# Later join and cache loads on GpSimd's queue in the attention stage of a decoder step

## The reference

```
for g in range(3):                       # (window, dilation) = (128, 1), (512, 4), (2048, 16)
    s = q_g . k_g * scale - slope * distance        # 129 keys per query, strided by the dilation
    m = max(s);  p = exp(s - m);  l = sum(p)
    o_g = p . v_g / l;  lse_g = m + log(l)
alpha = softmax over g of lse_g
o_a = sum over g of alpha_g * o_g                   # this is "the join"
```

## Time and profile before

| | us |
|---|---|
| median of 3 runs (3123.8 to 3127.46) | 3126.55 |
| the profiled execution | 3124.32 |
| span of its instructions | 3122.5 |
| TensorE busy in the span | 2919.9 (94%) |
| VectorE, ScalarE, GpSimd busy | 1361.6, 1085.1, 836.7 |

### The profile page before, as it was taken

One profiled execution on the slowest core, in us unless ns is written; L12 is line 12 of the kernel. 1 busy time (PEld: TensorE's weight loads), 2 busy tenths in 40 slices (PEclk: granted clock), 3 DMA queues, 4 the chain that ended last, 5 costly groups with the idle time before them and its releaser, 6 DMA issues. The chain is left out here.

```text
span 3122.5 us, 47274 instructions
## 1 busy us (share of the span) xinstructions
PE 2919.9 (94%) x18020; PEld 2609.9 (84%) x18020; DVE 1361.6 (44%) x3061; ACT 1085.1 (35%) x2165; POOL 836.7 (27%) x704
## 2 busy tenths in 40 slices
PE   7889999999999899999999999995979889589999
PEld 7778998888888799999999999993656656389999
DVE  2584334566544233343565645422434334433333
ACT  1343213444444333212444444442534434221110
POOL 0242333555422222232555533210011112040000
PEclk9999999999999999999999999997989797799999
DMA  6364432332322432322333232227676776353432
GB/s 195 95 178 137 125 95 77 105 98 92 104 99 88 166 113 94 111 84 88 95 100 102 90 100 94 98 71 263 240 262 224 254 246 212 123 194 109 126 119 86
DMA packets 385264, 417.90 MB, mean 134 GB/s; under 512 B 115600, under 2 KB 296080, under 8 KB 378384
## 3 DMA queue, kind: packets, MB, share of 16 engines
q1 hardware_dynamic: 378128, 406.24, 41.0%
q10 hardware_dynamic: 6912, 8.65, 0.8%
HBM read 284.11 MB, written 130.70 MB: 133 GB/s over the span
## 5 line engine op out<-in xcount | busy, mean ns | idle before, releaser
L667 PE MATMUL weave_bank<-h_high,w_high 128*128 128x352 f32 (+2 forms) x2240 | 819.8, 366 | 15.2 <-issue 11.4
L669 PE MATMUL weave_bank<-h_high,w_low 128*128 128x352 f32 (+2 forms) x2240 | 801.4, 358 | 0.0
L668 PE MATMUL weave_bank<-h_low,w_high 128*128 128x352 f32 (+2 forms) x2240 | 799.1, 357 | 0.0
L944 POOL TENSOR_TENSOR w_low<-weave_w_raw,w_high 128x512 fp32r<-128x512 f32 x284 | 379.9, 1349 | 771.1 <-ACT w_high L815 769.2
L667 PEld LDWEIGHTS weave_bank<-h_high,w_high 128*128 128x128 f32 x2240 | 427.0, 191 | 57.5 <-issue 14.7
L669 PEld LDWEIGHTS weave_bank<-h_high,w_low 128*128 128x128 f32 x2240 | 426.0, 190 | 40.4
L668 PEld LDWEIGHTS weave_bank<-h_low,w_high 128*128 128x128 f32 x2240 | 426.0, 190 | 39.7 <-issue 2.9
L679 PE MATMUL weave_bank<-w_high,h_high 128*128 128x256 f32 x1088 | 310.0, 285 | 0.0
L681 PE MATMUL weave_bank<-w_high,h_low 128*128 128x256 f32 x1088 | 306.7, 282 | 0.0
L680 PE MATMUL weave_bank<-w_low,h_high 128*128 128x256 f32 x1088 | 305.6, 281 | 0.0
L1671 ACT ACTIVATE mix_probs<-mix_scores,mix_o_out 128x256 f32<-128x256 f32 (+1 forms) x384 | 157.0, 454 | 319.2 <-DVE mix_o_out L1754 307.1
(11 more groups left out here) (229 smaller groups left out, 4860.6 us busy)
## 6 DMA issues: line engine op xcount, KB each, us to landing
weave_w_raw<-in_w_qkv SPq DMA_DIRECT2D x144, 256.0 KB, 2.9
mix_kv<-in_kT_c SPq DMA_DIRECT2D x24, 1024.0 KB, 7.6
mix_kv<-in_v_c SPq DMA_DIRECT2D x24, 1024.0 KB, 7.1
tail_gates<-scratch_gates SPq DMA_DIRECT2D x48, 352.0 KB, 3.2
weave_w_raw<-in_w_g SPq DMA_DIRECT2D x64, 256.0 KB, 3.0
weave_w_raw<-in_w_b SPq DMA_DIRECT2D x60, 256.0 KB, 2.8
scratch_sums<-mix_o_out SPq DMA_DIRECT2D x48, 264.0 KB, 6.0
mix_rows<-scratch_sums SPq DMA_DIRECT2D x24, 528.0 KB, 6.8
```

Source lines behind the costliest of these rows:

```text
L667: pe.matmul(dst, w_high[:, i, k, :], h_high[:, k, tok], start=(k == 0), stop=False)
L668: pe.matmul(dst, w_high[:, i, k, :], h_low[:, k, tok], start=False, stop=False)
L669: mm = pe.matmul(dst, w_low[:, i, k, :], h_high[:, k, tok], start=False, stop=(k == KD - 1))
L944: pool.tensor_tensor(w_part(w_low, p), w_raw[p % RAW][:, :, :], w_part(w_high, p), ALU.subtract).then_inc(w_low_done, 1)
```

## The change

Three things change in `phase_mix`. The parts of the samples all stand four blocks later (`at` begins at 8 in place of 4). For half 0 of the first three head pairs everything behind `load_rows` stands five blocks later (`later`), the load itself where it was. And `load_stage` moves from SP's list, unchanged, to GpSimd's: stages 0 and 1 at the top of the stage, right behind the clearing of the semaphores, the others in a loop over the blocks in which the weighted sums stand at their blocks.

```
-    at = lambda i, k: 4 + SPAN * i + k * SPAN // PARTS
+    at = lambda i, k: 8 + SPAN * i + k * SPAN // PARTS
...
-    turn_at = lambda jp, half: start(jp, half) + (12 if jp < PAIRS - 1 else 6 + 2 * half)
+    later = lambda jp, half: 5 if jp < PAIRS - 1 and half == 0 else 0
+    turn_at = lambda jp, half: start(jp, half) + later(jp, half) + (12 if jp < PAIRS - 1 else 6 + 2 * half)
     J_LOAD = {start(*x): x for x in J_HALVES}
-    J_LEAST = {start(*x) + 2: x for x in J_HALVES}
-    J_EXP = {start(*x) + 3: x for x in J_HALVES}
-    J_WEIGHT = {start(*x) + 4: x for x in J_HALVES}
-    J_SUM = {start(*x) + (7 if x == (PAIRS - 1, 1) else 5): x for x in J_HALVES}
+    J_LEAST = {start(*x) + later(*x) + 2: x for x in J_HALVES}
+    J_EXP = {start(*x) + later(*x) + 3: x for x in J_HALVES}
+    J_WEIGHT = {start(*x) + later(*x) + 4: x for x in J_HALVES}
+    J_SUM = {start(*x) + later(*x) + (7 if x == (PAIRS - 1, 1) else 5): x for x in J_HALVES}
...
             def _(sp):
-                def load_stage(s): ...
...
-                load_stage(0)
-                load_stage(1)
                 for n in range(END):
...
-                    if n in S_LOAD:
-                        load_stage(S_LOAD[n])
...
             def _(pool):
+                def load_stage(s): ...          # as before, with pool.wait_ge and pool.dma_start
...
                 nc.clear_and_free_semaphores(t["used"])
-                for jp in range(PAIRS - 1):
-                    for half in range(2):
-                        weighted_sums(pool, jp, half)
+                load_stage(0)
+                load_stage(1)
+                for n in range(END):
+                    if n in S_LOAD:
+                        load_stage(S_LOAD[n])
+                    if n in J_SUM and J_SUM[n][0] < PAIRS - 1:
+                        weighted_sums(pool, *J_SUM[n])
```

More of the change, by code:

```diff
@@ L1450, in store_sums @@
                     sp.dma_start(block_rows(dr["sums"][g, jp], g, quad), o_out[a % 2][:, 4 * quad:4 * quad + 4, :]).then_inc(sums_out[a % 2][quad // 2], 16)
[L1452 to L1468, removed]
                 def load_rows(jp, half):
@@ L1733, in _, with load_stage @@
             def _(pool):
-                nc.clear_and_free_semaphores(t["used"])
-                for jp in range(PAIRS - 1):
-                    for half in range(2):
-                        weighted_sums(pool, jp, half)
+                def load_stage(s):
+                    i, e = divmod(s, 8)
+                    x, nth = s % 2, s // 2
+                    if s >= 2:
+                        pool.wait_ge(stage_done, s - 1)
+                    for b in range(2):
+                        if e < 4:
+                            w = CH if e < 3 else P
+                            pool.dma_start(kv[x][b][:, :, 0:w], dr["kT_c"][2 * i + b, :, :, e * CH:e * CH + w]).then_inc(kv_in[x][b], 16)
+                        else:
+                            m = 4 * (e - 4)
+                            n = min(4, KEYS - m)
+                            pool.dma_start(kv[x][b][:, 0:n, :], dr["v_c"][2 * i + b][:, m:m + n, :]).then_inc(kv_in[x][b], 16)
+                        if e == 4:
+                            for g in range(G):
+                                new = dr[f"v_s{g}"].rearrange("j (b t) c -> b t j c", t=ST)
+                                pool.dma_start(v_new[b][g * ST:(g + 1) * ST], new[2 * i + b]).then_inc(vn_in[b], 16)
+                nc.clear_and_free_semaphores(t["used"])
+                load_stage(0)
[5 more added lines that the diff above has]
+                        weighted_sums(pool, *J_SUM[n])
             @block.vector
```

## The result

| | before | after |
|---|---|---|
| median of five runs each (range), us | 3123.8 (3122.3 to 3127.5) | 3099.4 (3091.2 to 3105.3) |
| ratio, 95% interval | | 0.9915 (0.9896 to 0.9934) |
| the profiled execution, us | 3124.3 | 3094.8 |
| length of blocks 16 to 186, us | 485.0 | 467.7 |

The account below looks back on a forecast made before the run. TensorE is at work for 94% of the span, so gains come only from its idle stretches, mainly the attention stage. 3124.3 - 45.5 - 12 - 10 + 8 = 3064.8 us, as a median 3067; range of 8 in 10: 3048 to 3102.

Parts of the forecast that it names:

- waits at the joins: Attention stage: VectorE's three waits for half 0's rows go, or shrink to about a us: 45.5 us off.
- give-back: Attention stage: chunks issued by GpSimd land late in bursts, and loads and weighted sums delay each other: 8 us lost.
- clock: Behind the three join waits TensorE no longer works at its lower level of 1.2 GHz: 12 us off.
- start: Start of the attention stage: fewer bytes must land before the first sample part, now at block 8: 10 us off.
- rival A: Joins: DMA engines are full anyway, so waits of 24 of 45.5 us stay; 3100 us, chance 0.20.
- If TensorE is idle elsewhere instead, this is lost again: Attention stage: caveat on the 12 us gained from TensorE's clock, lost if idle time arises elsewhere.
- the granted clock stays at 1.0 from about 2160 us: Sign that the forecast is right: TensorE's clock stays at 1.0 to the end of the attention stage's last job.
- The jobs without waits: The three jobs with join waits, at full clock without waits: 37.4, 38.9 and 35.8 us; excess 56 us.
- Rival B: TensorE's sample parts 2, 3, 10 and 11: GpSimd's queue brings chunks late; 3155 us at 6 us each, chance 0.07.
- GpSimd's issue: GpSimd's queue: issuing a cache chunk was taken as 2 us a DMA, 4 a chunk.

Follow-up runs that it names:

- the filling of the gaps in jobs 3 to 10: The kernel after, plus useless 0.55 us matmuls on TensorE in front of the instructions where its trace has gaps: 3077.9 us, ratio 0.9854.
- the fastest kernel: Against before: cache loads on GpSimd, join's half 0 five blocks later, its rows loaded six blocks earlier, sample parts from block 4: 3064.8 us, ratio 0.9805.
- loads on GpSimd alone: The kernel before with only the cache loads moved to GpSimd; join and sample parts as before: 3117.8 us, ratio 0.9971.
- early rows, base 8: The kernel after with the row loads of half 0 of the first three head pairs issued six blocks earlier: 3078.9 us, ratio 0.9846.
- all but GpSimd: The kernel before with the later join and sample parts from block 8, cache loads still on SP: 3099.9 us, ratio 0.9915.
- the filling that was to show it: The kernel before with 24, 18 and 18 useless matmuls in TensorE's three long join waits: 3118.5 us, ratio 0.9983.
- the fastest kernel with the filling: The fastest kernel plus one or two useless matmuls at each of its eight short gaps: 3065.8 us, ratio 0.9816.
- all but the parts' move: The kernel after with the sample parts from block 4, as before: 3091.4 us, ratio 0.9886.

## Why the prediction was wrong

The terms of the sum, as the profiled executions show them (blocks 16 to 186, and the start):

| term | forecast | measured | from |
|---|---|---|---|
| waits at the joins | -45.5 | -31.2 | TensorE's wait behind VectorE, 42.4 to 11.2 |
| give-back | +8 | +7.4 | other idle time of TensorE, 49.3 - 42.4 = 6.9 to 25.5 - 11.2 = 14.3 |
| clock | -12 | +4.4 | busy time, 435.7 to 442.2, less 2.1 for moved sample parts |
| start | -10 | -6.6 | block 16 is 9.7 earlier, 3.1 of it a part that now stands behind it |
| rest | 0 | -3.5 | moved parts and the end, not followed |
| sum | -59.5 | -29.5 | |

By the parts' move, part 3 of the first pair has come into this stretch (3.1 us: four such parts hold 12.5 us of matmuls) and the closing part of the last has left it (1.0 us).

Of the 30.0 us that are missing, 16.4 are the clock's, 14.3 the joins' and 3.4 the start's; 4.1 came back elsewhere. The median, 3099.4, lies in the range of 8 in 10 (3048 to 3102) only because that range took in rival A.

- **The step that failed: the clock.** "If TensorE is idle elsewhere instead, this is lost again" stands in the prediction, and so does a give-back of 8 us; I did not put the two together. The give-back came, in the size forecast, most of it as gaps of 0.9 to 2.0 us. Behind gaps of this kind the clock fell; one, of 1.28 us in block 63, alone cost 6 to 11 us. The sentence "the granted clock stays at 1.0 from about 2160 us" fell: it was at 0.5 for 81.9 us between blocks 16 and 186, against 102.4 before, and with TensorE at work for 75.3 us of that, against 70.5. That the clock costs this time is shown by the filling of the gaps in jobs 3 to 10: -21.5 us, with the matmuls themselves 27 us shorter. After's own five runs agree with it, as they stand in the order of their mean granted clock: 3091.2 us at 0.965, 3094.8 at 0.964, 3099.4 at 0.963, 3100.3 at 0.962, 3105.3 at 0.960.
- **The size of the loss was about right, the belief that this change collects it was wrong.** The jobs without waits were estimated at 37.4, 38.9 and 35.8 us; in the fastest kernel jobs 3, 6 and 9 take 36.5, 36.9 and 38.0. That kernel gets 485.0 - 430.1 = 54.9 us in the middle, where I had 45.5 + 12 - 8 = 49.5.
- **The joins: the second step that was off.** Two of the three waits went as said. The first stayed with 7.7 us. VectorE asked 27.5 us after SP's first issue (2254.0), as forecast, but the rows took 35.2 us where I had 21 to 27. I had let at most 2.1 MB of chunks go ahead of the rows and counted their flight at the burst's rate from SP's first issue; in fact SP stood 5.5 us at the sums' store behind the job's inputs, and 2.62 MB of chunks then went between the rows. Also 3.6 of VectorE's 45.5 us were never idle time of TensorE (17.0, 12.3 and 12.6 idle).
- **Rival A** gave 3100, and its mechanism is half of the answer. The engines are full and a second queue adds little: loads on GpSimd alone are worth 7.3 us. The Trainium skill, "DMA: Bandwidth & Descriptors", section "Issuing engines are not separate DMA queues", says that DMAs of all issuing engines run on the same 16 engines; the trace agrees: beside each other the two queues have 66.8 and 39.7% of the 16 engines and 339 GB/s, and SP's alone had 112.9% and 325 GB/s. But two of the three waits it wanted to stay did not, since the later join gave the rows five blocks more; 9.2 us of VectorE's waits stayed in place of its 24. Its time came out by luck: the clock lost what its waits did not.
- **The start** gave 6.6 us in place of 10; 2.6 us are lost at VectorE's first score, where job 0's inputs share the engines with the chunks, as the prediction allowed for.
- **Rival B** did not happen: TensorE waits 3.3 us in two waits for chunks. GpSimd's issue, put at 2 us a DMA, is 0.75.
- What stays open: why a gap brings the clock down at one time and not at another, as the same gap of 1.28 us did in after and in "early rows, base 8" (27.3 us at 0.50 in both) and not in "all but GpSimd"; what part the sample parts' small matmuls have in it, behind which the clock also fell without a gap; and what part of the 18.6 us by which TensorE's busy time in before exceeds the fastest kernel's comes from the long waits alone; the filling that was to show it was too short.

## What to carry to other kernels

Count idle time of TensorE twice: by its length, and by what the clock does behind it; a gap of one microsecond can cost several times its own length, and in another kernel nothing. Before a load is moved to another queue, look whether the engines have room at that moment: here the same rows, issued six blocks earlier from the same queue into a half idle stretch, gave 47 us, and a second queue 7. A change in three parts should be timed in its parts: here one carried the gain, one added 6 us at most, and one took some 8 away.

## What the runs showed of the hardware

- Behind a gap of 1.28 us TensorE's granted clock stood at 0.50 for 27.3 us of uninterrupted work, in after and in "early rows, base 8"; in "all but GpSimd" it stayed at 1.00 behind the same gap. A gap of 1.38 us at the turn of block 77 was followed by 3.4 us at 0.50 in after, and by none in the fastest kernel.
- The clock also fell with no gap over 0.1 us, 1.9 to 2.0 us behind 48 matmuls of 128x8 (four times, 6.8 to 13.7 us at 0.50; "loads on GpSimd alone", and the fastest kernel with the filling).
- Work that is useless can shorten a program: 19 us of it on TensorE gave 21.5 us back (3099.4 to 3077.9).
- A DMA's issue on GpSimd took 0.75 us for a 1 MB tile of keys and 0.55 us for a tile of values; before, on SP, two took 1.22 us. The keys' chunks landed after 10.0 us by median, against 7.6.
- With GpSimd's chunks beside them, three DMAs of 528 KB on SP's queue took 17.8 to 24.4 us from first issue to landing at the joins' half 0 (loads on GpSimd alone, all but the parts' move, and after), against 11.1 to 11.9 in before. The rate of the engines was about the same, 339 against 325 GB/s.
